# The attention layer's row factor moved behind the value, query and key products, and the state space layer's end worked by groups

## What is computed

```python
# layer 0, around attention
x = x + 0.5 * rmsnorm(swiglu(rmsnorm(x, g[0]), ...), g[1])
h = rmsnorm(x, g[2])                 # x * r * g[2], r one factor per token
q, k, v = jnp.split(h @ w_qkv, 3, axis=-1)
...
# layer 1, the state space mixer: per chunk of tokens a scan of states xs, then
y = jnp.einsum('ghp,bcgp->bcgh', c, xs).real + d_g * u_c
z = jax.nn.gelu(y) @ w_glu + b_glu
return z[..., :D_MODEL] * jax.nn.sigmoid(z[..., D_MODEL:])
```

## Time and profile before

| what | value |
|---|---|
| three timed runs | 1666.51, 1667.3, 1667.78 us, median 1667.3 |
| profiled execution, its own time | 1664.28 us |
| its span, first to last instruction | 1662.5 us |
| TensorE busy | 1632.9 us, 98% |
| VectorE busy | 1101.2 us, 66% |
| ScalarE busy | 927.6 us, 56% |
| GpSimd busy | 165.8 us, 10% |
| share of the chain that ended last | TensorE 89%, VectorE 5%, ScalarE 4% |

### The profile page before, as it was taken

How to read it: one execution, slowest core, us unless ns; L and a number is a source line. 1 busy time by engine, 2 the same in 40 slices (tenths; PEclk the granted TensorE clock), 3 DMA queues, 4 the chain that set the end, 5 groups by cost and what they waited for, 6 DMA issues and landing times.

```text
span 1662.5 us, 22547 instructions
## 1 busy us (share of the span) xinstructions
PE 1632.9 (98%) x8995; PEld 1372.6 (83%) x8995; DVE 1101.2 (66%) x1567; ACT 927.6 (56%) x1559; POOL 165.8 (10%) x240
## 2 busy tenths in 40 slices
PE   9999999999999999999999999999999999999997
PEld 7888899788888877888878888788889889788886
DVE  5555667788877664869775556755567776665555
ACT  6555556655567585452465556655555444655555
POOL 0000001128301111900000000000000000000000
PEclk9999999999999999999999999999999999999999
DMA  6765443555555544451555545565544333554552
GB/s 235 252 209 186 181 165 127 179 195 191 189 191 190 206 174 152 174 181 52 190 184 182 198 178 190 192 219 199 179 176 178 140 116 128 184 203 177 196 184 102
DMA packets 50297, 295.93 MB, mean 178 GB/s; under 512 B 6072, under 2 KB 12688, under 8 KB 16528
## 3 DMA queue, kind: packets, MB, share of 16 engines
q1 hardware_dynamic: 49744, 293.86, 49.4%
q0 software_dynamic: 160, 0.52, 0.1%
q10 hardware_dynamic: 288, 0.11, 0.0%
HBM read 293.39 MB, written 1.09 MB: 177 GB/s over the span
## 4 chain that ended last, share of the span: by engine, by line
PE 89%; DVE 5%; ACT 4%; issue 1%; POOL 0%; DMA 0%; POOLq 0%; DVEq 0%; ACTq 0%
PE PS L2134 84%; PE PS L2356 2%; DVE wlo L1325 1%; PE PS L2279 1%; PE PS L2137 1%; ACT SC L964 1%; ACT whi L747 1%; PE PS L2571 0%; ACT wk L787 0%; DMA raw<-in_w 0%; DVE SC L1910 0%; DVE SC L1612 0%; DVE st L1596 0%; ACT wk L814 0%; DVE SC L1593 0%
## 5 line engine op out<-in xcount | busy, mean ns | idle before, releaser
L1331 DVE SCALAR_TENSOR_TENSOR wlo<-raw,ct,whi 128x512 fp32r<-128x512 f32 (+1 forms) x552 | 425.1, 815 | 259.2 <-ACT whi L751 259.2
L2134 PE MATMUL PS<-whi,xhi 128*128 128x512 f32 (+1 forms) x1312 | 505.6, 395 | 6.0 <-DVE wlo L1331 2.2
L751 ACT ACTIVATE whi<-raw,ct 128x512 fp32r<-128x512 f32 (+1 forms) x552 | 377.5, 734 | 224.2 <-PE PS L2134 170.6
L2134 PE MATMUL PS<-wlo,xhi 128*128 128x512 f32 (+1 forms) x1312 | 495.5, 387 | 0.0
L1325 DVE TENSOR_TENSOR wlo<-raw,whi 128x1024 fp32r<-128x1024 f32 x240 | 296.6, 1244 | 215.9 <-ACT whi L747 215.5
L2134 PE MATMUL PS<-whi,xlo 128*128 128x512 f32 (+1 forms) x1312 | 405.5, 387 | 0.0
L747 ACT ACTIVATE whi<-raw 128x1024 fp32r<-128x1024 f32 x240 | 251.8, 1057 | 258.4 <-PE PS L2134 192.1
L2134 PEld LDWEIGHTS PS<-whi,xhi 128*128 128x128 f32 x1312 | 246.0, 188 | 60.9 <-ACT xhi L822 4.1
L2134 PEld LDWEIGHTS PS<-whi,xlo 128*128 128x128 f32 x1312 | 246.4, 188 | 51.4
L2134 PEld LDWEIGHTS PS<-wlo,xhi 128*128 128x128 f32 x1312 | 246.6, 188 | 47.4
L2134 PE MATMUL PS<-whi,hhi 128*128 128x512 f32 x544 | 173.3, 392 | 0.1
(11 more groups left out here) (282 smaller groups left out, 1508.7 us busy)
## 6 DMA issues: line engine op xcount, KB each, us to landing
raw<-in_w SPq DMA_DIRECT2D x263, 1024.0 KB, 4.8
gr<-in_rows SPq DMA_DIRECT2D x14, 512.0 KB, 3.9
SC<-scratch SPq DMA_DIRECT2D x5, 512.0 KB, 5.7
X<-in_x SPq DMA_DIRECT2D x2, 512.0 KB, 5.1
raw<-in_w SPq DMA_DIRECT2D x2, 512.0 KB, 6.7
SC<-scratch SPq DMA_DIRECT2D x4, 256.0 KB, 5.1
xn<-in_sc SPq DMA_DIRECT2D x2, 512.0 KB, 6.1
SC<-scratch SPq DMA_DIRECT2D x1, 1024.0 KB, 8.8
```

The source lines that it names most:

```text
L751: e = a.activation(hi[:, f], src[:, f], ACT.Copy, scale=ct[:, c:c + 1])
L1331: e = v.scalar_tensor_tensor(lo[:, f], src[:, f], ct[:, c:c + 1], hi[:, f].bitcast(f32), MUL, SUB)
L2134: return pe.matmul(o, l, r, start=start, stop=stop)
```

## The change

Entry of attention. xn becomes X g2 without r2, made right behind each half of X (`add_x_times_g2`), so the transposes need no r2. The value copies take r2 as ScalarE's scale; queries and keys are stored by channel with tokens along the row, and need r2 as a row: VectorE makes a matrix with r2 of the partition in every column (`factors`), TensorE transposes it into bank 2, VectorE copies it to rk, and `query_key`, now on VectorE, multiplies by rk. All fills between ffn0 and v0 are gone, and the squares of X move behind the second half's transposes. The orders of ScalarE and VectorE there are written out.

State space layer. In the first channel half VectorE's first turned product moves between the scans; TensorE's fill is gone, `own`, `from_states` and the Gelu go by groups, the third and fourth term change places, and the second half's `own` is split around the first products of glu1. In the second channel half the Gelu's transposes stand ahead of the products that they stood between.

The diff, cut to its core:

```diff
             def settle(k):
-                if k in FOLDED or k == STORED:
+                if k in FOLDED + DEFER or k == STORED:
...
-            def query_key(h):
-                b = 4 + h % 2
-                q.wait_ge(s_used, ATTN_AT + QK_AT[h] + 2)
-                a.activation(turned(q_t[:, h, :]), in128(PS[:, b, 0:S]), ACT.Copy, scale=0.125)
-                a.activation(k_t[:, h, :], PS[:, b, S:2 * S], ACT.Copy).then_inc(s_qk, 1)
...
-                    a.activation(vv[:, h, out], PS[:, bank + h, cols], ACT.Copy).then_inc(s_vv, 1)
+                    q.wait_ge(s_r2, n_one(1, h))
+                    a.activation(vv[:, h, out], PS[:, bank + h, cols], ACT.Copy, scale=r2[1][h]).then_inc(s_vv, 1)
...
-                linear("v0", 4, head=4, tail=0, finish=lambda: evict_hi(1, 1))
+                def turned_1():
+                    evict_hi(1, 1)
+                    squares2(1, 0)
+                    squares2(1, 1)
+
+                linear("v0", 4, head=4, tail=0, finish=turned_1)
...
-            settle(1, {1: lambda: released(0)})
+            squares(1, 0)
+            released(0)
+            squares(1, 1, (0,))
+            evict_hi(1, 0, (0,))
+            squares(1, 1, (1,))
+            use(ATTN_AT - 1)
+            evict_hi(1, 0, (1,))
+            use(ATTN_AT)
             attention()
...
+            def add_x_times_g2(k, h):
...
+                for i, f in enumerate((LO, HI)):
+                    v.scalar_tensor_tensor(X[:, h, f], yg_of(k, h)[:, f], r1[k][h], X[:, h, f], MUL, ADD).then_inc(s_X, 1)
+                    q.wait_ge(s_X, n_x(k, h, i))
+                    v.tensor_tensor(xn[:, h, f], X[:, h, f], g2[:, f], MUL).then_inc(s_xn, 1)
...
+            def factors():
+                q.wait_ge(s_tr, n_tr(1, 1))
+                for h in range(2):
+                    q.wait_ge(s_r2, n_one(1, h))
+                    v.tensor_scalar(xn[:, h, 768:896], idt[:, :], 0.0, r2[1][h], MUL, ADD).then_inc(a_rk, 1)
+
+            def query_key(h):
+                if h == 0:
+                    q.wait_ge(a_rkT, 1)
+                    v.tensor_copy(rk, PS[:, 2, 0:S].rearrange("p (h t) -> p h t", h=2)).then_inc(a_rk, 1)
+                    q.wait_ge(a_rk, 3)
+                q.wait_ge(s_used, ATTN_AT + QK_AT[h] + 2)
+                b = PS[:, 4 + h % 2, :]
+                v.scalar_tensor_tensor(turned(q_t[:, h, :]), in128(b[:, 0:S]), 0.125, rk, MUL, MUL)
+                v.tensor_tensor(in128(k_t[:, h, :]), in128(b[:, S:2 * S]), rk, MUL).then_inc(a_key, 1)
...
                 for j in range(4, 30):
+                    if j == 5:
+                        factors()
                     heads(j)
...
                     q.wait_ge(s_xr, (3, 5)[m])
+                    if m:
+                        low(0, (0,))
                     link(v.tensor_tensor(t[:, :, 0, f], t[:, :, 0, f], b[:, :, 1, f], ADD))
+                    link(v.tensor_tensor(t[:, :, 1, f], t[:, :, 1, f], b[:, :, 0, f], SUB))
                     if m:
-                        low(0)
-                    link(v.tensor_tensor(t[:, :, 1, f], t[:, :, 1, f], b[:, :, 0, f], SUB))
+                        low(0, (1,))
...
                         v.tensor_tensor_scan(*flat_, 0.0, MUL, ADD).then_inc(s_sc, 1)
+                        if m == 0:
+                            q.wait_ge(s_sc, k + 1)
+                            v.tensor_tensor(t[:, :, k, :], b[:, :, k, :], co[:, :, k, :], MUL).then_inc(s_st, 1)
                     q.wait_ge(s_sc, 2 * m + 2)
                     if m == 0:
-                        for k in range(2):
-                            v.tensor_tensor(t[:, :, k, :], b[:, :, k, :], co[:, :, k, :], MUL).then_inc(s_st, 1)
...
                     for h in range(2):
+                        if h and by_half is not None:
+                            transposed(1, 1)
...
-                            if low is False and h == 0 and n == 2:
-                                fill_in(tr_bank(1, 1, 0), ATTN_AT, 4)
-                                transposed(1, 1)
...
                 values("v0", slice(0, 512), 0, range(4), True, 1)
+                q.wait_ge(a_rk, 2)
+                for h in range(2):
+                    e = pe.transpose(PS[:, 2, 128 * h:128 * h + 128], xn[:, h, 768:896], idt[:, :])
+                e.then_inc(a_rkT, 1)
...
-                own(0)
-                fill_in(2, GLU_AT, 5)
-                from_states(0)
                 for g in range(2):
-                    gelu_turned(0, g)
-                own(1)
-                for k in range(4):
-                    q.wait_ge(s_glo, k // 2 + 1)
-                    run([part(u1, k)], 2, False, step=4)
+                    own(0, g)
+                for k in range(2):
+                    q.wait_ge(s_st, k + 1)
+                    for g in range(2):
+                        from_states(0, g, k, chunk[0][:, k])
+                q.wait_ge(s_st, 4)
+                from_states(0, 0, 0, turn_b[0][:, 1])
+                q.wait_ge(s_st, 3)
+                from_states(0, 0, 1, turn_b[0][:, 0]).then_inc(s_ys, 1)
+                from_states(0, 1, 0, turn_b[0][:, 1])
+                gelu_turned(0, 0)
+                from_states(0, 1, 1, turn_b[0][:, 0]).then_inc(s_ys, 1)
+                own(1, 0)
+                gelu_turned(0, 1)
+                for g in range(2):
+                    q.wait_ge(s_glo, g + 1)
+                    run([part(u1, 2 * g), part(u1, 2 * g + 1)], 2, False, step=4)
+                    if g == 0:
+                        own(1, 1)
...
                 for g in range(2):
+                    gelu_turned(1, g)
                     second_half(2 + g, 0, False)
-                    gelu_turned(1, g)
```

More of the change, by code:

```diff
@@ L345, in program @@
         g8 = b1t[:, 128:256]
+        rk = xn[:, :, 896:1024]
         lam, le = stat(4), stat(2)
@@ L2093, in vector @@
             bg.drain()
-            take_turns(1, steps, {2: lambda: released(0)})
+            gate_or_low(1, 0)
+            times_g(1, 0)
+            add_x_times_g2(1, 0)
+            released(0)
+            evict_lo(1, 0, (0,))
+            gate_or_low(1, 1)
+            times_g(1, 1)
+            use(ATTN_AT - 1)
+            evict_lo(1, 0, (1,))
+            use(ATTN_AT)
+            add_x_times_g2(1, 1)
             attention()
@@ L2240, in meanwhile @@
                 b = tr_bank(k, h, 0)
-                if h and k not in DEFER:
+                if h:
                     if k == PLACED:
@@ L2249, in meanwhile @@
                 turn_idle(k, b, s_X, n_x(k, h, 1), 9 if k == PLACED else 4)
-                if k not in DEFER:
-                    turn_idle(k, b, s_X, n_x(k, 1, 1), 8 if k == PLACED else 4)
+                turn_idle(k, b, s_X, n_x(k, 1, 1), 8 if k == PLACED else 4)
             def transposed(k, h):
@@ L2256, in transposed @@
                 q.wait_ge(l_id, 16)
-                if k not in FOLDED and not (h and k in DEFER):
+                if k not in FOLDED + DEFER:
                     meanwhile(k, h)
@@ L2589, in s5, with own @@
                 q.wait_ge(s_kb, 2)
-                def own(m):
+                def own(m, g):
                     q.wait_ge(s_xr, (3, 5)[m])
-                    for i in range(16):
+                    for i in range(8 * g, 8 * g + 8):
                         r = kb[:, 16 * m + i, :, :].rearrange("p v n -> p (v n)")
@@ L2600, in own, with from_states @@
                                 mm_add(o, l, r)
-                def from_states(m, half=None):
-                    whole, turned_ = chunk[m], turn_b[m]
-                    if m == 0:
-                        terms = ((1, 0, whole[:, 0]), (2, 1, whole[:, 1]), (3, 1, turned_[:, 0]), (4, 0, turned_[:, 1]))
-                    else:
-                        terms = ((5 + 2 * half, 0, whole[:, 0]), (6 + 2 * half, 1, whole[:, 1]))
-                    for ready, k, state in terms:
-                        q.wait_ge(s_st, ready)
-                        for i in range(8 * half, 8 * half + 8) if m else range(16):
-                            e = mm_add(yb(m, i), state[:, i, :], cst[:, k, 16 * m + i, :, :].rearrange("p v n -> p (v n)"))
-                            if i % 8 == 7 and ready == terms[-1][0]:
-                                e.then_inc(s_ys, 1)
+                def from_states(m, g, k, state):
+                    for i in range(8 * g, 8 * g + 8):
+                        e = mm_add(yb(m, i), state[:, i, :], cst[:, k, 16 * m + i, :, :].rearrange("p v n -> p (v n)"))
+                    return e
                 def gelu_turned(m, g):
```

37 lines of the change are left out of this document (24 added, 13 removed).

## The result

The changed kernel is slower: 1667.2 us (median of 21 runs, 1665.2 to 1668.7) against 1664.5 us for the kernel before on the same chips (21 runs, 1662.9 to 1667.8). The ratio is 1.0014, 95% interval 1.0009 to 1.0020, so between 1.5 and 3.3 us are lost. The forecast was 1.5 us gained. Its time, 1665.8, stood on the three runs that were known then, whose median lay 2.8 above that of the 21, so the difference is what has to be compared. That 1667.2 lies inside the stated 1663.0 to 1669.0 is luck of that base: as a difference the range went from 4.3 gained to 1.7 lost, and 2.7 were lost.

What follows compares the result with a forecast made beforehand. TensorE was taken as the bound, busy 1632.9 of 1662.5 us. Attention's 1.2 lost and 1.2 back sum to 0, the state space layer gains 1.5: 1667.3 less 1.5 is 1665.8 us, range 1663.0 to 1669.0.

Steps and rivals of the forecast that it cites:

- The entry: Entry of attention: v0 ends 2.8 us earlier, but the late row factor starts the first query product 1.2 us later.
- the row factor is not late: Rival at attention's entry: squares or splits end sooner and the entry keeps its 2.8 us; 1663.0 or 1661.8; chance 0.14.
- the four squares ahead of the splits: ScalarE at attention's entry: four squares end at 214.4 and delay its halves, so VectorE's four splits end at 220.0.
- Inside attention: Attention's head loop: query and key copies leave ScalarE, so 0.6 of each of two TensorE waits goes, 1.2 us back.
- VectorE never became the bound: Rival in the head loop: VectorE's query and key products cost double, 1.9 us a head, giving 1669.0; chance 0.05.
- The state space layer: End of that layer: 2.6 us of fills and waits removed, less 1.1 of new costs, 1.5 us gained.
- the two new waits: End of the state space layer: the third product and own of the second half each wait 0.5 us.
- the cost of going to and fro between shapes: End of the state space layer: four more changes of shape on TensorE cost some 0.15 us.
- I take nothing: TensorE's 3.8 us pause at attention's entry: no clock fall counted in the sum, 2.65 us kept for the range.
- the rival: Attention's entry: the clock falls in TensorE's 3.8 us pause and costs 2.65 us, giving 1668.5; chance 0.11.
- The last sentence of the prediction: Signs of being wrong: early first query product, double-length products behind the pause, VectorE without idle time before splits, waits in untouched stages.

Runs made afterwards that it cites:

- the kernel with all together: Against the changed kernel: factors ahead of the splits, row factor's copy and first head's query/key before the fifth half unit's split, small products in three entry waits; 1659.17 us, 0.9967.

## Why the prediction was wrong

**The entry: right in its sum, a little short, and one link of the path was not the one that held.** v0's second half starts at 210.62 plus 0.60, 211.2 (forecast 211.1), the factors at 220.3 (220.0), the first query product at 221.0 (220.6). The row factor is late because it stands behind the four splits, as forecast: putting the factors ahead of the splits removed the pause, and "the row factor is not late" is out. But the four squares ahead of the splits are not what held it. ScalarE's third high half, and with it VectorE's third split, had to wait:

```profile
212.96 0.63 ACT L814 ACTIVATE wk<-X 128x512 f32<-128x512 f32 x1
...
213.59 1.99 ACT L747 ACTIVATE whi<-raw 128x1024 fp32r<-128x1024 f32 x2
216.35 2.00 ACT L747 ACTIVATE whi<-raw 128x1024 fp32r<-128x1024 f32 x2 [0.77 <-PE PS L2188]
```

The profile names TensorE, whose last product of v0 ends at 216.32, but the transfer of these weights (number 37, issued at 209.68) lands at 216.32 too. In the kernel with all together it lands at 215.85, the high half starts at 215.87, and v0 goes on until 216.47: it is the transfer that is waited for. With the squares alone the four splits would have ended near 219.3 (214.66 and four of 1.16, an estimate) instead of 219.80. That the factors came so close to the forecast is in part luck.

**Inside attention: right.** 1.37 came back where 1.2 was forecast, and moving the two copies to VectorE did it alone: from the first scores to ffn1 it takes 89.14 in that kernel's trace and 90.50 before, and the ratio gives 1.5, though its interval reaches to no change. The new products are 0.42 and 0.41 each, so VectorE never became the bound.

**The state space layer: right in kind, 1.0 for 1.5.** Of the two new waits the first came (0.43 as listed, 0.60 by the starts of the products) and the second did not. Two things were missing. One is a third, short wait of about 0.14, for VectorE's second product by the cosine, which ends at 772.48; TensorE's seventeenth product starts at 772.53. With it and the longer first wait the first 64 products from the states take 3.85 (770.65 to 774.93, less the listed wait) where 64 took 3.54 (769.35 to 772.89, before). The other is the cost of going to and fro between shapes, which I had put at 0.15: four Gelu transposes among products from the states take 0.58 (777.70 to 778.28) where 0.36 was counted, and the last sixteen products 1.12 (778.28 to 779.40), where a quarter of 3.6 is 0.9.

**The clock: the step that failed first.** "I take nothing" for a pause of 3.8 us. It came to 3.93, and the granted clock fell in both traces that have this pause: 3.41 us at half with 1.5 lost in the one, 6.83 with 2.1 lost in the other; between the kernels with fills and with small products in the pause it makes 1.5 by the traces and 1.75 to 2.1 by the medians. So the rival named the mechanism, and its 2.65 was too much: that price is from a stretch of 5.49 us at the program's start. Against it I held that nothing had fallen in waits up to 1.9 in the earlier trace rows. The page could not have shown it, since a fall of 3.41 us leaves a 9 in its slice, as the page after shows; the trace before indeed has no fall there, but that was one execution. The same two pauses of 1.7 and 1.9 us near 1305 and 1362 stand in eleven traces of these kernels, and behind one of them the clock fell in six, for 3.4 us each time; so what one execution doesn't show is no proof. Part of the scatter between runs goes with this: of the 77 runs of before beside the experiments, the 28 with a mean granted clock of 0.999 have a median of 1663.67, the 36 with 0.997 one of 1665.85. The Trainium skill (TensorE: Matmul & The Clock Gate, Part 1: The HAM clock gate), by which an idle engine goes back to the lower clock, had the sign right here: with it the sum was a loss.

**What no step had: the fetches of instructions.** The last sentence of the prediction names waits in stages that the change doesn't touch as a sign of being wrong, and they are there: 1.39 in ffn1 and 0.70 at the end, 2.1 together. The packets of 16 KB come one to 256 instructions of TensorE (71 of them for 8976 products and as many weight loads), so taking out sixteen fills and adding two transposes moved the places at which they are fetched. In the five kernels with that count ahead of ffn1 a fetch of 16 KB lies inside transfer 113, which takes 5.57 to 6.24 us; in the seven with the old count, or two products more, it lies ahead of it, and the transfer takes 4.66 to 4.87. Adding small products at the entry moved it out, adding them later did not, and moved the later ones out. The Trainium skill (Runtime: NRT & Kernel Launch, Instruction fetch mechanics) has instructions refilled in blocks of 16 KiB, 256 instructions; the packets of 0.02 MB agree with the size. Not every transfer that meets a fetch is late; those are that met it early. In the twelve traces 28 transfers of weights that had the queue nearly to themselves (at most 1.12 MB moved meanwhile) met a fetch that began 1.0 to 3.5 us after their issue, and all 28 took 5.4 to 6.4 us; with the fetch 4 us or more after the issue the median of 405 is 4.82 (5 of them above 5.2), and without a fetch that of 1727 is 4.78. How one packet of about 1 us holds up a whole transfer by as much is not shown.

Put together, without the two chance terms of the profiled execution (-0.60 and +1.56): 1.65 + 1.58 - 1.37 - 1.02 + 1.39 + 0.70 - 0.12 = **+2.8**, where 2.7 was measured. That is 4.3 from the forecast of 1.5 gained: 1.6 from the first query product to the first scores, nearly all of it the clock, 2.1 the fetches, and 0.6 small misses in the other stages. With only the clock corrected the forecast would have been about no change; the two microseconds beyond that are the fetches.

## What to carry to other kernels

A fill product that looks like waste can hold the clock, and it counts as instructions too: before taking it out, ask how long the pause behind it becomes, and look afterwards at stages far away for transfers that land a microsecond late with an instruction packet inside them. Where a new value is late on one engine, let the consumer do first what doesn't need it, or let the producer do it ahead of work that nobody waits for yet; either was worth about 5 us here. Judge differences of 0.1% by stage lengths in the traces beside the median, since a chance fall of the clock alone moves one execution by about 1.5.

## What the runs showed of the hardware

- A pause of TensorE of 2.2 us with sixteen 128x8 products ahead of it (1.84 us) ended in the lower clock as one of 3.9 did; sixteen 128x512 products in the same place kept the upper one.
- Slow stretches came in two lengths, 3.41 and 6.83 us, and pauses of 1.7 to 1.9 us were followed by one in six of eleven traces. A stretch of 3.41 us cost 1.5 to 1.6 us where the two could be compared, a little less than half of it.
- A fetch of 16 KB of instructions that began 1.0 to 3.5 us after the issue of a 1 MB transfer of weights went with a landing at 5.4 to 6.4 us instead of 4.8 (28 of 28 transfers, in twelve traces), one 4 us or more after the issue mostly did not (5 of 405 above 5.2). TensorE's instruction count ahead of the place decided where the fetch fell.
